# Order of the conditioning multiply-adds, and of the first item's passes, in a one-core fp32r block kernel

## The chip, the cores and the metric

The kernel runs on one NeuronCore of a Trainium2 chip. The metric is the device time of one execution in microseconds (us), the median over several runs. TensorE is called PE here, VectorE DVE, ScalarE ACT, GpSimd POOL and SyncE SP.

## What is computed

Two model blocks on one sequence of 512 tokens and 1024 channels, all in float32. Cut to what matters here:

```python
def _swiglu(h, w_gu, w_down):
    gate, up = jnp.split(h @ w_gu, 2, axis=-1)
    return (jax.nn.silu(gate) * up) @ w_down
...
x = x + 0.5 * _swiglu(_rmsnorm(x, ffn1_norm), ffn1_w_gu, ffn1_w_down)
h = _rmsnorm(x, mix_norm)
u_hy, u_rw, g_hy, g_rw = jnp.split(h @ w_in, split_at, axis=-1)
...
x = x + merged @ w_out
x = x + 0.5 * _swiglu(_rmsnorm(x, ffn2_norm), ffn2_w_gu, ffn2_w_down)
...
cond = jax.nn.silu(c)
ada = cond @ ada_w[l] + ada_b[l]
...
y = jnp.square(jax.nn.relu(h @ w1)) @ w2
x = x + g2[:, None, :] * rmsnorm(y, norm_g[l, 3])
```

`cond @ ada_w` and `cond @ kv_ada_w` are the conditioning: a vector of 1024 times a wide matrix. They depend on no token, so the kernel spreads them over other work. The rest (a Hyena branch, an RWKV-7 scan, an mLSTM, an attention) lies between the stages that the change touches.

## The kernel before

The text names functions and lines of the profiled kernel. Channels lie on the partitions; a weight matrix is processed by `dense` (L518), which is called five times: `ffn1`, `hy_in`, `mix`, `mlp0` and `mlp1`. Each call gets a list of steps: `Gemm` (a weight matrix), `Norm` (an RMS norm that makes the input of the next Gemm) and `Cut` (the same without a norm).

**Items.** `lay_out` (L430) cuts each Gemm into items of about 1 MB of weights: 8 blocks of 128 rows by two output tiles of 128 columns. Every product is made in three passes, because a float32 number is cut into a high and a low fp32r part: high weight by high input, high weight by low input, low weight by high input. So an item has 8 x 2 x 3 = 48 matmuls of 128 x 512 (L658, L660, L664). Two slots hold raw, high and low weights, so item i+2 uses the slots of item i, and also the PSUM banks of item i where a group is one item.

**What each engine does for an item i,** in program order:

- SP loads the raw weights of item n when item n-2 has its low part (L591 to L604).
- ACT: `take_out(i)` (silu of the gate tile, L757, or relu, L763), then `upper(i+2)`, the high part of the weights (L732), which waits for the last matmul of item i.
- DVE: `take_out(i)` (for swiglu and sqrelu two operations to a tile, L845 and L846; for "add" one, L861), then `lower(i+2)`, the low part of the weights (L836), and then, in a Gemm with a side job, `side_half(st, i)` (L887): four multiply-adds of one half of a conditioning block (L897, L900), each waiting for the one before.
- POOL: `side_load(st, i)` (L993, the DMA of L999), then the low part of item i's result (L1017), which waits for `take_out(i)`. `side_load` waits for `side_half(i-1)`, since there is one buffer `sraw`, and it stands in POOL's queue behind item i-1's low part.
- PE: the products; `bank_free` waits for DVE's `take_out(i-2)`; and after each even item but the first, and at the end of the Gemm, `side_sums` (L691): column sums of the accumulator `acc` (L697). A `side_half` of an even item starts `acc` anew and waits for the sums of the pair before, which PE makes behind the products of that same item.

Gemms with side jobs are: up (22 items, swiglu) and down (12 items, "add") of `ffn1` and of the second feed-forward in `mix`, each with blocks of 384 columns, and up1 (8 items, sqrelu) and down1 (8 items) of `mlp0`, with blocks of 256 columns. At the end of each, `side_take` (L904) adds the bias on DVE.

**The start of a stage.** The first item of a Gemm behind a Norm or Cut is "fresh": PE takes the input parts one by one as they come. It waits for the item's low weights before anything:

```python
for t in ts:
    bank_free(it, t)
pe.wait_ge(lo_ready, it.n + 1)
for k in ks:
    wait_hi(pe, st.parts, k)
    for t in ts:
        nc.tensor.matmul(ps[:, it.banks[t], :], w(h, k, t), xh[:, k, :], ...
        nc.tensor.matmul(ps[:, it.banks[t], :], w(l, k, t), xh[:, k, :], start=False, stop=False)
```

Where `dense` starts with a Norm or Cut, ACT makes `upper(items[0])` and DVE `lower(items[0])` ahead of the input parts (for a Norm that makes its own sums, ACT does it behind the squares). In `hy_in` the Norm is "known": the root was kept from an earlier stage, so its input parts need only x. The first items of `ffn1`, `hy_in`, `mlp0` and `mlp1` are fresh; that of `mix` is not.

Of the kernel before, what the change touches and what calls it, by code (L numbers as in the profile page):

```python
# [517 lines left out]
def dense(nc, e, tag, steps, buf):  # L518
# [6 lines left out]
    with ExitStack() as s:  # L525
# [80 lines left out]
        @block.tensor  # L606
        def _(pe):
            def bank_free(it, t):
                if it.first and it.earlier[t] is not None:
                    was, u = it.earlier[t]  # L610
                    if was.gemm.kind in ("copy", "tokens"):
                        pe.wait_ge(act_out, was.out[u])
                    else:
                        pe.wait_ge(dve_out, was.out[u])

            def products(it):
                st, h, l = it.gemm, slot(wh, it), slot(wl, it)
                xh, xl = st.x
                ks, ts = range(it.k0, it.k1), range(len(it.js))
                w = lambda of, k, t: of[:, k - it.k0, t * P:(t + 1) * P]  # L620
                pe.wait_ge(hi_ready, it.n + 1)
                if st.kind == "tokens":
                    for t in ts:
                        bank_free(it, t)
                        tok = slice(t * P, (t + 1) * P)
                        for k in ks:
                            nc.tensor.matmul(ps[:, t, :], xh[:, k, tok], h[:, k - it.k0, :],
                                             start=it.first and k == it.k0, stop=False)
                            nc.tensor.matmul(ps[:, t, :], xl[:, k, tok], h[:, k - it.k0, :], start=False, stop=False)
                        if t == 0:  # L630
                            pe.wait_ge(lo_ready, it.n + 1)
                        for k in ks:
                            last = nc.tensor.matmul(ps[:, t, :], xh[:, k, tok], l[:, k - it.k0, :], start=False,
                                                    stop=it.last and k == it.k1 - 1)
                        if it.last:
                            last.then_inc(tile_done, 1)
                elif it.fresh:
                    for t in ts:
                        bank_free(it, t)
                    pe.wait_ge(lo_ready, it.n + 1)  # L640
                    for k in ks:
                        wait_hi(pe, st.parts, k)
                        for t in ts:
                            nc.tensor.matmul(ps[:, it.banks[t], :], w(h, k, t), xh[:, k, :],
                                             start=it.first and k == it.k0, stop=False)
                            nc.tensor.matmul(ps[:, it.banks[t], :], w(l, k, t), xh[:, k, :], start=False, stop=False)
                    for k in ks:
                        wait_lo(pe, st.parts, k)
                        for t in ts:
                            last = nc.tensor.matmul(ps[:, it.banks[t], :], w(h, k, t), xl[:, k, :], start=False,  # L650
                                                    stop=it.last and k == it.k1 - 1)
                            if it.last and k == it.k1 - 1:
                                last.then_inc(tile_done, 1)
                else:
# [3 lines that stand above are left out]
                            nc.tensor.matmul(ps[:, it.banks[t], :], w(h, k, t), xh[:, k, :],  # L658
                                             start=it.first and k == it.k0, stop=False)
                            nc.tensor.matmul(ps[:, it.banks[t], :], w(h, k, t), xl[:, k, :], start=False, stop=False)  # L660
                        if t == 0:
                            pe.wait_ge(lo_ready, it.n + 1)
                        for k in ks:
                            last = nc.tensor.matmul(ps[:, it.banks[t], :], w(l, k, t), xh[:, k, :], start=False,  # L664
                                                    stop=it.last and k == it.k1 - 1)
                        if it.last:
                            last.then_inc(tile_done, 1)
                if not it.last:
                    last.then_inc(item_done, 1)

            def sum_tile(st, k):

                pe.wait_ge(squared, st.square[k])
                if k == 0 and st.order > 1:
                    pe.wait_ge(rooted, st.order - 1)
                for g in range(TT):
                    gs = slice(32 * g, 32 * g + 32)
                    last = nc.tensor.matmul(sums[gs, 0:P], e.ones[:, 0:32], sq[:, st.square[k] % 3, g * P:(g + 1) * P],
                                            start=k == 0, stop=k == st.n - 1)
                last.then_inc(summed, 1)  # L680

            def spread_root(st):
                pe.wait_ge(inverted, st.order)
                if st.saves > 0:
                    pe.wait_ge(saved, st.saves)
                for g in range(TT):
                    row = e.ident[:, 32 * g:32 * g + 1].to_broadcast([P, P])
                    last = nc.tensor.matmul(rs[:, g * P:(g + 1) * P], row, sd[:, 1, :], start=True, stop=True)
                last.then_inc(spread, 1)

            def side_sums(st, n):  # L691

                pe.wait_ge(side_step, DT * (st.side_at + n + 1))
                cols = st.side[1] // P
                for j in range(cols):
                    at = st.column_at + n * cols + j
                    last = nc.tensor.matmul(sps[:, at:at + 1], acc[:, j * P:(j + 1) * P], e.ones[:, 0:1],  # L697
                                            start=True, stop=True)
                last.then_inc(side_sum, 1)

            for st in steps:
                if isinstance(st, Gemm):
                    fed = st.feeds if isinstance(st.feeds, Norm) else None
                    for i, it in enumerate(st.items):
                        products(it)
                        if fed and i > 0 and st.items[i - 1].last:
                            for j in st.items[i - 1].js:
                                sum_tile(fed, j)
                        if st.side and i > 0 and i % 2 == 0:
                            side_sums(st, i // 2 - 1)  # L710
                    if fed:
                        for j in st.items[-1].js:
                            sum_tile(fed, j)
                    if st.side:
                        side_sums(st, len(st.items) // 2 - 1)
                elif isinstance(st, Norm) and not st.known:
                    if st.fed is None:
                        for k in range(st.n):
                            sum_tile(st, k)
                    spread_root(st)  # L720

        @block.scalar
        def _(act):
# [74 lines left out]
            for st in steps:  # L798
# [7 lines left out]
                if isinstance(st, Norm) and not st.known:  # L806
# [3 lines left out]
                    if started == 0:  # L810
                        upper(items[0])
                    root(st)
                elif started == 0:
                    upper(items[0])
                if st.kind == "parts" and (isinstance(st, Norm) or st.fed is None):
                    for k in range(st.n):
                        first_part(st, k)
                if isinstance(st, Norm) and st.root is not None and not st.known:
                    act.wait_ge(pieces, st.piece[-1])
                    nc.scalar.activation(st.root, rs[:, :], ACT.Copy).then_inc(saved, 1)  # L820
# [7 lines left out]
        def _(dve):  # L828
# [136 lines left out]
            for st in steps:  # L965
                if isinstance(st, Gemm):
                    for i, it in enumerate(st.items):
                        if it.last:
                            take_out(it)
                        if following(it) and not late(it):  # L970
                            lower(following(it))
                        if st.side:
                            side_half(st, i)
                    if st.side:
                        side_take(st)
                    continue
                if started == 0:
                    lower(items[0])
                if isinstance(st, Norm):
                    pieces_of(st)  # L980
                if st.kind == "parts":
                    for k in range(st.n):
                        if not st.on_pool[k]:
# [2163 lines left out]
```

## Time and profile before

| | |
|---|---|
| median of 3 runs | 3242.55 us (3241.94 to 3242.68) |
| the profiled execution, its own time | 3243.93 us |
| its span, first to last instruction | 3242.1 us |
| PE busy (matmuls; ends are modelled) | 2813.5 us, 87% of the span |
| DVE busy | 1592.8 us, 49% |
| ACT busy | 873.1 us, 27% |
| POOL busy | 400.5 us, 12% |
| mean granted PE clock | 0.916 of full speed |
| DMA | 272.78 MB, mean 84 GB/s |

Shares are averages over stages with different limits. In the stages of `dense` PE works without gaps through most items and waits at their starts and ends. A busy time of a matmul includes its way through the array: back-to-back matmuls of 128 x 512 start every 0.23 us at full clock though each is shown with 0.39 us.

### The profile page before, as it was taken

The numbers are of one execution on the slowest core, as the hardware profiler recorded it, in microseconds if no ns is written. First come the engines' busy times: TensorE is split into PE (matmuls) and PEld (weight loads), VectorE is DVE, ScalarE is ACT, GpSimd is POOL, SyncE is SP. The second block draws the span as 40 slices with busy tenths as digits, with TensorE's granted clock in tenths as the row PEclk, the third lists the DMA queues.
The fourth block names the chain that finished last, engine by engine and source line by source line (L and its number), as shares of the span: only waits on it lengthen the run. The fifth ranks groups of instructions, "written<-read, shape, count | busy, mean of one in ns | idle before, by whom it ended". The sixth has DMA issues, their size and how long they took to land. (4 is left out here: it accounts for less than half of the span.)

```text
span 3242.1 us, 40247 instructions
## 1 busy us (share of the span) xinstructions
PE 2813.5 (87%) x17297; PEld 2199.6 (68%) x17297; DVE 1592.8 (49%) x2116; ACT 873.1 (27%) x1114; POOL 400.5 (12%) x376
## 2 busy tenths in 40 slices
PE   7999997788587769999998979589999659889998
PEld 5887874777462458788876853368877446668886
DVE  5554456666655453565545224644263535353342
ACT  3221234111134112322213233332221333432221
POOL 1111001111001110111100001212030100021010
PEclk8999998899798789999998987789999779989999
DMA  5554530000020022355543310123243210223231
GB/s 159 160 159 153 163 100 21 3 3 3 28 73 26 0 65 85 98 162 168 167 141 123 100 34 2 52 65 107 95 137 121 53 44 2 78 67 103 91 104 52
DMA packets 267299, 272.78 MB, mean 84 GB/s; under 512 B 10559, under 2 KB 248102, under 8 KB 266927
## 3 DMA queue, kind: packets, MB, share of 16 engines
q1 hardware_dynamic: 251760, 208.32, 21.0%
q0 software_dynamic: 15360, 61.87, 5.8%
q8 instruction: 137, 2.24, 0.3%
q14 instruction: 42, 0.34, 0.0%
HBM read 268.07 MB, written 2.10 MB: 83 GB/s over the span
## 5 line engine op out<-in xcount | busy, mean ns | idle before, releaser
L836 DVE TENSOR_TENSOR mlp_wl<-mlp_raw,mlp_wh 128x2048 fp32r<-128x2048 f32 x74 | 189.9, 2566 | 290.7 <-ACT mlp_wh L732 290.7
L836 DVE TENSOR_TENSOR mix_wl<-mix_raw,mix_wh 128x2048 fp32r<-128x2048 f32 (+2 forms) x66 | 153.1, 2320 | 244.6 <-ACT mix_wh L732 244.5
L658 PE MATMUL mix_ps<-h_mix_hi,mix_wh 128*128 128x512 f32 x624 | 245.1, 393 | 9.2 <-ACT mix_wh L732 9.2
L660 PE MATMUL mix_ps<-h_mix_lo,mix_wh 128*128 128x512 f32 x624 | 243.7, 390 | 0.0
L732 ACT ACTIVATE mix_wh<-mix_raw 128x2048 fp32r<-128x2048 f32 (+2 forms) x66 | 117.6, 1781 | 246.0 <-PE mix_ps L664 162.1
L732 ACT ACTIVATE mlp_wh<-mlp_raw 128x2048 fp32r<-128x2048 f32 x74 | 140.5, 1899 | 154.0 <-PE mlp_ps L664 88.8
L658 PE MATMUL ffn_ps<-h_rw_hi,ffn_wh 128*128 128x512 f32 x448 | 175.2, 391 | 0.0
L660 PE MATMUL ffn_ps<-h_rw_lo,ffn_wh 128*128 128x512 f32 x448 | 174.3, 389 | 0.0
L664 PE MATMUL mix_ps<-h_mix_hi,mix_wl 128*128 128x512 f32 x624 | 154.2, 389 | 0.0
L658 PE MATMUL mlp_ps<-view,mlp_wh 128*128 128x512 f32 x384 | 150.1, 391 | 0.0
L660 PE MATMUL mlp_ps<-view,mlp_wh 128*128 128x512 f32 x384 | 149.5, 389 | 0.0
L836 DVE TENSOR_TENSOR ffn_wl<-ffn_raw,ffn_wh 128x2048 fp32r<-128x2048 f32 (+1 forms) x42 | 106.1, 2526 | 80.7 <-ACT ffn_wh L732 80.7
L658 PEld LDWEIGHTS mix_ps<-h_mix_hi,mix_wh 128*128 128x128 f32 x624 | 117.8, 189 | 34.2 <-ACT mix_wh L732 9.6
L1017 POOL TENSOR_TENSOR view<-mlp_f,view 128x512 fp32r<-128x512 f32 x64 | 86.4, 1351 | 424.6 <-DVE mlp_f L846 424.6
L660 PEld LDWEIGHTS mix_ps<-h_mix_lo,mix_wh 128*128 128x128 f32 x624 | 117.8, 189 | 24.1
L664 PEld LDWEIGHTS mix_ps<-h_mix_hi,mix_wl 128*128 128x128 f32 x624 | 117.1, 188 | 24.3
L732 ACT ACTIVATE ffn_wh<-ffn_raw 128x2048 fp32r<-128x2048 f32 (+1 forms) x42 | 78.7, 1874 | 177.2 <-PE ffn_ps L664 149.9
L658 PE MATMUL mlp_ps<-h_ml_hi,mlp_wh 128*128 128x512 f32 x296 | 115.7, 391 | 0.0
L660 PE MATMUL mlp_ps<-h_ml_lo,mlp_wh 128*128 128x512 f32 x296 | 115.3, 389 | 0.0
L658 PE MATMUL mlp_ps<-h_mla_hi,mlp_wh 128*128 128x512 f32 x288 | 112.3, 390 | 0.0
L845 DVE SCALAR_TENSOR_TENSOR view<-mlp_ps,mlp_f 128x512 fp32r<-128x512 f32 x64 | 44.2, 691 | 138.3 <-ACT mlp_f L763 138.3
L660 PE MATMUL mlp_ps<-h_mla_lo,mlp_wh 128*128 128x512 f32 x288 | 112.1, 389 | 0.0
(560 smaller groups left out, 6111.5 us busy)
## 6 DMA issues: line engine op xcount, KB each, us to landing
mlp_raw<-in_mlp_w SPq DMA_DIRECT2D x64, 1024.0 KB, 5.3
ffn_sraw<-in_ada_w POOLq DMA_DIRECT2D x34, 768.0 KB, 5.3
ffn_raw<-in_ffn_w_gu SPq DMA_DIRECT2D x44, 512.0 KB, 5.2
mix_raw<-in_ffn_w_gu SPq DMA_DIRECT2D x44, 512.0 KB, 4.6
mix_sraw<-in_ada_w POOLq DMA_DIRECT2D x22, 768.0 KB, 5.2
mix_raw<-in_a_w_in SPq DMA_DIRECT2D x12, 1024.0 KB, 5.3
mix_sraw<-in_kv_ada_w POOLq DMA_DIRECT2D x12, 768.0 KB, 4.9
ffn_raw<-in_w_in SPq DMA_DIRECT2D x8, 1024.0 KB, 5.3
```

The source lines that it names most:

```text
L658: nc.tensor.matmul(ps[:, it.banks[t], :], w(h, k, t), xh[:, k, :], start=it.first and k == it.k0, stop=False)
L660: nc.tensor.matmul(ps[:, it.banks[t], :], w(h, k, t), xl[:, k, :], start=False, stop=False)
L664: last = nc.tensor.matmul(ps[:, it.banks[t], :], w(l, k, t), xh[:, k, :], start=False, stop=it.last and k == it.k1 - 1)
L732: nc.scalar.activation(slot(wh, it), slot(raw, it), ACT.Copy).then_inc(hi_ready, 1)
L836: nc.vector.tensor_tensor(slot(wl, it), slot(raw, it), slot(wh, it).bitcast(F32), ALU.subtract)\
L845: nc.vector.scalar_tensor_tensor(st.dst[0][:, j, :], ps[:, bank, :], op0, f[:, u % 2, :], op1, ALU.mult)
L1017: nc.gpsimd.tensor_tensor(d, f[:, 2 + u % 2, :], st.dst[0][:, j, :].bitcast(F32), ALU.subtract).then_inc(low, 1)
```

## The change

Four edits, all in `dense`.

1. PE, first item of a call (`it.n == 0`) if fresh: the wait for the low weights moves behind the pass of high weights by high inputs, and the low weights by high inputs become a pass of their own, which comes second.
2. ACT, `dense` that starts with a known Norm (only `hy_in`): `upper(items[0])` moves from ahead of the eight high input parts to behind the fourth.
3. DVE, the same stage: `lower(items[0])` moves behind the eight products of the Norm (`pieces_of`).
4. DVE, every item with a side job: `side_half` moves from behind `lower` to ahead of `take_out`.

```diff
@@ products, fresh item
                     for t in ts:
                         bank_free(it, t)
-                    pe.wait_ge(lo_ready, it.n + 1)
+                    if it.n > 0:
+                        pe.wait_ge(lo_ready, it.n + 1)
                     for k in ks:
                         wait_hi(pe, st.parts, k)
                         for t in ts:
                             nc.tensor.matmul(ps[:, it.banks[t], :], w(h, k, t), xh[:, k, :],
                                              start=it.first and k == it.k0, stop=False)
-                            nc.tensor.matmul(ps[:, it.banks[t], :], w(l, k, t), xh[:, k, :], start=False, stop=False)
+                            if it.n > 0:
+                                nc.tensor.matmul(ps[:, it.banks[t], :], w(l, k, t), xh[:, k, :], start=False, stop=False)
+                    if it.n == 0:
+                        pe.wait_ge(lo_ready, 1)
+                        for k in ks:
+                            for t in ts:
+                                nc.tensor.matmul(ps[:, it.banks[t], :], w(l, k, t), xh[:, k, :], start=False, stop=False)
@@ scalar
-                elif started == 0:
+                elif started == 0 and not isinstance(st, Norm):
                     upper(items[0])
                 if st.kind == "parts" and (isinstance(st, Norm) or st.fed is None):
                     for k in range(st.n):
                         first_part(st, k)
+                        if started == 0 and isinstance(st, Norm) and st.known and k == st.n // 2 - 1:
+                            upper(items[0])
@@ vector
                     for i, it in enumerate(st.items):
+                        if st.side:
+                            side_half(st, i)
                         if it.last:
                             take_out(it)
                         if following(it) and not late(it):
                             lower(following(it))
-                        if st.side:
-                            side_half(st, i)
                     if st.side:
                         side_take(st)
                     continue
-                if started == 0:
+                known = isinstance(st, Norm) and st.known
+                if started == 0 and not known:
                     lower(items[0])
                 if isinstance(st, Norm):
                     pieces_of(st)
+                if started == 0 and known:
+                    lower(items[0])
```

DVE's queue in the first items of `ffn1`'s up Gemm, before (`wl` is the low weights, `acc` the conditioning accumulator, `ffn_f` what ACT's silu wrote and the second result part; a line "x3" is three of them):

```order
L836 TENSOR_TENSOR ffn_wl<-ffn_raw,ffn_wh 128x2048
L897 TENSOR_SCALAR ffn_acc<-ffn_sraw,cond 128x384
L900 SCALAR_TENSOR_TENSOR ffn_acc<-ffn_sraw,cond,ffn_acc 128x384 x3
L845 SCALAR_TENSOR_TENSOR view_194<-ffn_ps,ffn_f 128x512
L846 SCALAR_TENSOR_TENSOR ffn_f<-ffn_ps,ffn_f 128x512
L836 TENSOR_TENSOR ffn_wl<-ffn_raw,ffn_wh 128x2048
L900 SCALAR_TENSOR_TENSOR ffn_acc<-ffn_sraw,cond,ffn_acc 128x384 x4
```

The same queue with the change (line numbers are 9 higher; the first line is the low part of item 1's weights):

```order
L845 TENSOR_TENSOR ffn_wl<-ffn_raw,ffn_wh 128x2048
L906 TENSOR_SCALAR ffn_acc<-ffn_sraw,cond 128x384
L909 SCALAR_TENSOR_TENSOR ffn_acc<-ffn_sraw,cond,ffn_acc 128x384 x3
L854 SCALAR_TENSOR_TENSOR view_194<-ffn_ps,ffn_f 128x512
L855 SCALAR_TENSOR_TENSOR ffn_f<-ffn_ps,ffn_f 128x512
L845 TENSOR_TENSOR ffn_wl<-ffn_raw,ffn_wh 128x2048
L909 SCALAR_TENSOR_TENSOR ffn_acc<-ffn_sraw,cond,ffn_acc 128x384 x4
```

The cyclic order of the three groups is the same; what moved is where an item begins. Before, the four lines on `acc` between two pairs of L845 and L846 belong to the item whose pair is ahead of them; now they (L906, L909) belong to the item whose pair is behind them, and that pair can't run until they have.

POOL's queue in the same place with the change, which is as before but for line numbers (the DMA loads the conditioning block, the other operation is the low part of an item's result):

```order
L1011 DMA ffn_sraw<-in_ada_w 128x4x384
L1029 TENSOR_TENSOR view_195<-ffn_f,view_194 128x512
L1011 DMA ffn_sraw<-in_ada_w 128x4x384
L1029 TENSOR_TENSOR view_195<-ffn_f,view_194 128x512
L1011 DMA ffn_sraw<-in_ada_w 128x4x384
```

Nothing moved here: each load stands behind the low part of the item before, as it did.

ACT's queue at the start of `hy_in` with the change (before, the first `hy_in_wh` stood ahead of all eight `h_mix_hi`; the last two lines are the take-out of item 0):

```order
L787 ACTIVATE h_mix_hi<-view_8977 128x512 x4
L739 ACTIVATE hy_in_wh<-hy_in_raw 128x2048
L787 ACTIVATE h_mix_hi<-view_8977 128x512 x4
L739 ACTIVATE hy_in_wh<-hy_in_raw 128x2048
L755 ACTIVATE view_8971<-hy_in_ps,cols 128x512
L759 ACTIVATE view_8972<-hy_in_ps 128x512
```

Four input parts are now made ahead of the weights. PE's first 32 matmuls there alternated between `hy_in_wh` and `hy_in_wl`; now sixteen read `hy_in_wh`, and then sixteen `hy_in_wl`.

## Rows read from the trace of the kernel before

**Rows 1.** waits of PE over the whole execution: waited for, us in total, times, longest.

```profile
PE mlp_ps L644 <- DVE mlp_wl L836: 42.7, 2, 32.2
```

**Rows 2.** timeline, ffn1's up Gemm, items 1 to 3: start, duration (us), instruction, [idle before].

```profile
63.31 2.57 DVE L900 SCALAR_TENSOR_TENSOR ffn_acc<-ffn_sraw,cond,ffn_acc 128x384 f32<-128x384 f32 x4
...
69.25 0.73 PE L697 MATMUL ffn_sps<-ones,ffn_acc 128*128 128x1 f32 x6
69.45 0.69 DVE L845 SCALAR_TENSOR_TENSOR view<-ffn_ps,ffn_f 128x512 fp32r<-128x512 f32 x1 [3.58 <-PE ffn_ps L664]
70.06 0.68 DVE L846 SCALAR_TENSOR_TENSOR ffn_f<-ffn_ps,ffn_f 128x512 f32<-128x512 f32 x1
71.46 2.81 DVE L836 TENSOR_TENSOR ffn_wl<-ffn_raw,ffn_wh 128x2048 fp32r<-128x2048 f32 x1 [0.72 <-ACT ffn_wh L732]
74.19 0.41 DVE L897 TENSOR_SCALAR ffn_acc<-ffn_sraw,cond 128x384 f32<-128x384 f32 x1
74.64 1.93 DVE L900 SCALAR_TENSOR_TENSOR ffn_acc<-ffn_sraw,cond,ffn_acc 128x384 f32<-128x384 f32 x3
...
70.83 1.28 POOL L1017 TENSOR_TENSOR view<-ffn_f,view 128x512 fp32r<-128x512 f32 x1 [3.89 <-DVE ffn_f L846]
76.86 0.77 POOL L999 DMA_DIRECT2D ffn_sraw<-in_ada_w  x1 [4.74 <-DVE ffn_acc L900]
```

**Rows 3.** timeline, the end of ffn1's up Gemm (item 21).

```profile
283.03 0.69 DVE L845 SCALAR_TENSOR_TENSOR view<-ffn_ps,ffn_f 128x512 fp32r<-128x512 f32 x1 [4.72 <-PE ffn_ps L664]
...
290.10 1.44 PE L697 MATMUL ffn_sps<-ones,ffn_acc 128*128 128x1 f32 x6 [7.10 <-DVE ffn_acc L900]
```

**Rows 4.** timeline, mlp0's up0 Gemm, item 0, DVE and then POOL.

```profile
2174.99 0.69 DVE L845 SCALAR_TENSOR_TENSOR view<-mlp_ps,mlp_f 128x512 fp32r<-128x512 f32 x1 [2.13 <-ACT mlp_f L763]
...
2177.39 2.42 DVE L836 TENSOR_TENSOR mlp_wl<-mlp_raw,mlp_wh 128x2048 fp32r<-128x2048 f32 x1
2177.62 3.34 POOL L1017 TENSOR_TENSOR view<-mlp_f,view 128x512 fp32r<-128x512 f32 x1
```

**Rows 5.** DVE at 40 us; loads' landing: ffn1, those of 40, 55, 276 us, mlp0.

```profile
38.09 4.26 DVE L918 TENSOR_TENSOR h_rw_lo<-view,h_rw_hi 128x512 fp32r<-128x512 f32 x4
...
DMA to landing us min/median/max: 4.9/5.3/6.7
...
ffn_sraw<-in_ada_w POOLq DMA_DIRECT2D x1, 768.0 KB, 5.4
...
ffn_sraw<-in_ada_w POOLq DMA_DIRECT2D x1, 768.0 KB, 6.7
...
ffn_sraw<-in_ada_w POOLq DMA_DIRECT2D x1, 768.0 KB, 4.9
...
DMA to landing us min/median/max: 3.9/4.6/5.8
```

**Rows 6.** column sums of mlp0 (first and last start), and the end of its up1 Gemm.

```profile
L697 PE MATMUL mlp_sps<-ones,mlp_acc x32: 168/250/370, 2370.2 to 2530.6; 128*128 128x1 f32 x32
...
2431.66 2.03 DVE L900 SCALAR_TENSOR_TENSOR mlp_acc<-mlp_sraw,cond,mlp_acc 128x256 f32<-128x256 f32 x4
2433.75 1.01 PE L697 MATMUL mlp_sps<-ones,mlp_acc 128*128 128x1 f32 x4 [7.46 <-DVE mlp_acc L900]
```

**Rows 7.** timeline, start of hy_in.

```profile
887.82 1.91 ACT L732 ACTIVATE hy_in_wh<-hy_in_raw 128x2048 fp32r<-128x2048 f32 x1 [13.66 <-DMA hy_in_raw<-in_w_in]
...
893.53 0.77 PE L644 MATMUL hy_in_ps<-h_mix_hi,hy_in_wh 128*128 128x512 f32 x1 [25.71 <-ACT h_mix_hi L780]
```

**Rows 8.** timeline, start of mlp0.

```profile
2091.01 4.25 ACT L786 ACTIVATE h_ml_hi<-view 128x512 fp32r<-128x512 f32 x8
...
2093.53 0.76 PE L644 MATMUL mlp_ps<-h_ml_hi,mlp_wh 128*128 128x512 f32 x1 [32.18 <-DVE mlp_wl L836]
```

**Rows 9.** timeline, the end of ffn1's down Gemm.

```profile
422.17 0.83 PE L697 MATMUL ffn_sps<-ones,ffn_acc 128*128 128x1 f32 x6 [1.40 <-DVE ffn_acc L900]
...
423.44 0.95 DVE L936 RECIPROCAL ffn_sd<-ffn_sd 128x128 f32<-128x128 f32 x1
```

## The prediction

> **What bounds the kernel now.** I read the page first: PE is busy 87% of the span, everything else half of it or less, so what counts is where PE waits and what comes last there. Then the waits of PE: it waits for the low weights of a first item twice [rows 1]; the start of `hy_in` and the ends of the Gemms with a side job show in the timeline. In the middle of a Gemm there is no wait worth the name: 19 items of the up Gemm take 283.03 - 69.45 = 213.6 us, 11.24 us each [rows 2, 3]. So the question for each edit is what it does to a start or an end, and whether a chain on another engine becomes longer than an item.
>
> **Starts.** In `hy_in` the raw weights land, ACT makes the high part at 887.82 in 1.91 us, DVE the low part behind it, then the first product of the Norm and its high part, and PE starts at 893.53 [rows 7]. With the change the products and four high input parts are made while the weights are still on their way, and PE needs only the high weights: 887.82 + 1.91 + 0.1 = 889.8. After that PE doesn't wait again: the first matmul of a part takes 0.77 us there [rows 7], and a part is made in 0.53 us (eight in 4.25 [rows 8]). Saved: 3.7 us. In `mlp0` ACT starts the high input parts at 2091.01, 4.25 / 8 = 0.53 us each and the first ends at about 2091.6, while PE waits for the low weights until 2093.53 [rows 8]: saved 1.9 us, and the same in `mlp1`, the second of the two waits [rows 1]. In `ffn1` PE waits for the Norm, not for the weights: nothing. The low weights take DVE 2.4 us [rows 4] and are ready long before PE's second sixteen. Sum of the starts: -7.5 us.
>
> **The side job moved ahead of the take-out.** This is the edit that decides. At first sight it only gains: at the end of up PE waits 7.10 us for the last multiply-add, because it comes behind take-out and low weights [rows 3], and 7.46 us in `mlp0` [rows 6]. But it closes a loop that was open. The load of the next conditioning block stands in POOL's queue behind the low part of this item's result; that waits for the take-out; the take-out now waits for this item's multiply-adds; and these wait for their load. Nothing in this loop waits for PE once it is late. Its links for a swiglu item:
>
> - four multiply-adds: 74.19 to 76.57 = 2.38 us for an even item, 2.57 us for an odd one [rows 2];
> - take-out: 69.45 to 70.74 = 1.29 us, and POOL starts 0.1 us later [rows 2];
> - the low part on POOL: 1.28 us [rows 2], but that is with DVE idle or behind it. DVE's low weights wait for ACT there until 71.46, so POOL is first, and DVE takes 2.81 us beside it. With the change an even item's take-out ends at least 4.2 us behind the item (0.7 us of column sums, 2.4, 1.3), when ACT's high weights are long ready, so DVE starts the low weights in the same moment and is 0.2 us ahead of POOL. The trace has this very sequence once in `mlp0`: DVE starts at 2177.39 and takes 2.42 us, POOL starts at 2177.62 and takes 3.34 us instead of 1.28 [rows 4]. I take 3.34;
> - issue to landing of the load: 5.3 us median, 4.9 to 6.7; of the 17 loads of this Gemm that I read one by one, from the one of 55 us to the one of 276 us, the mean is 5.5 [rows 5]. A chain adds means, so I take 5.5; the weight load is now issued 1.2 us ahead of it, not 2.6;
> - 0.15 us for POOL's step to the load and DVE's start on it, an estimate.
>
> A link is 2.38 + 1.29 + 0.1 + 3.34 + 5.5 + 0.15 = 12.8 us from an even to an odd item, 13.0 us back: 12.85 against the 11.24 of PE. So the side job falls behind by 1.6 us an item. After some five or six items the take-out of item i ends later than PE is done with item i+1, and then PE waits for its banks; for the end that makes no difference, since PE can't go on to down before the last sums. The loop's last free point is item 2, whose multiply-adds start behind the sums at 69.25 + 0.73 = 70.0 [rows 2]. From there 10 even and 9 odd links are 10 x 12.76 + 9 x 12.95 = 244.2 us, and the last multiply-adds 2.57: 316.7, where PE's last sums started at 290.10 [rows 3]. **+26.6 us**, and the same in the second feed-forward: +53.2. The bounds are those of the load: with 4.9 us 19 x 0.6 = 11.4 us less, +15.2 each; with 6.2 us, nearer to the longest rows, 13.3 more, +39.9 each. With 5.3, the median, it is 3.8 less.
>
> Up1 of `mlp0` has eight items, two tiles each: multiply-adds 2.0, take-out 2177.39 - 2174.99 + 0.1 = 2.5 us, POOL's second low part 0.1 + 3.34 [rows 4], load 4.9 (median 4.6, range 3.9 to 5.8 [rows 5]; seven loads have this mean), 0.15: 13.0 us. From item 2, 2370.2 + 0.6 = 2370.8 [rows 6], five links and 2.03 us lead to 2437.8, where it was 2433.75: +4.1 us, bounds +1 and +8.
>
> **Where the side job has no such loop.** In down and down1 POOL has nothing but the loads, so a link is multiply-adds plus load, 2.4 + 5.5 + 0.4 = 8.3 us, less than an item, and the even items stay tied to PE's sums. There the last multiply-adds are ready before the item ends, DVE's two additions come next at once, and the root's reciprocal, which stood behind sums that had waited 1.40 us [rows 9], comes earlier; the take-out of the first tile now comes late, behind the multiply-adds, and eats about 0.3 us. I take -1.1, -1.1 and -0.8, in sum -3.0 us; bounds -5 and, if the last load is late, +3. DVE's added delay of the low weights (2.4 us of 11) costs nothing: the next use is an item later.
>
> **Sum**, against the profiled execution: 3243.93 - 7.5 + 53.2 + 4.1 - 3.0 = 3290.7 us. The median of the runs is 1.4 us below that execution, so 3289 us, 1.4% slower.
>
> **A rule against the trace.** The load issued at 40 us had DVE busy with operations on two SBUF inputs all around it (38.09 to 42.35) and landed in 5.4 us, as the others do [rows 5]. The Trainium skill, page "SBUF — State Buffer", section "SBUF: two separate sides", states that a DMA from GpSimd's queue gets no descriptors written while DVE holds the shared port in a two-port mode. By that rule the loads of the down Gemms, now issued right when DVE starts its low weights, would land some 2 us later.
>
> **Rivals.**
>
> 1. *POOL keeps its turn* (faster). If the low part of the result starts ahead of DVE's low weights, or isn't held up, it takes 1.28 us, the link is 10.7 us and below PE's 11.24: the loop never closes, item 21's multiply-adds end at 272.0 + 10.7 + 2.57 = 285.3, and PE saves 4.8 us at each swiglu end and about 5 in `mlp0`. Total 3242.5 - 7.5 - 9.6 - 5 - 3: 3217 us. It decides at a hold-up of POOL below some 0.5 us. For it: POOL was first in every side item so far. Against: rows 4, and that the order of the queues fixes who is first. 11%.
> 2. *The loads get longer* since weights and conditioning now travel together: above 6.2 us the sum is over 3320 us, each 0.1 us more adds 4 us. Against: the transfers were overlapping before. 9%.
> 3. *DVE holds up the loads of down*: the last multiply-adds end 1.5 to 2 us behind the last item instead of ahead, the ends of down and down1 lose 1 us each instead of gaining one: +6, 3295 us. This is the rule above; the load of 40 us speaks against it. 4%.
> 4. *Shorter loads*, at or below 4.9 us, since the load now starts with DVE idle: below 3262 us, in the extreme nothing but the starts' gain against a small loss. 4%, half of it within 0.2%.
>
> My forecast has the remaining 72%.
>
> **Numbers.** A measurement of this kernel can tell about 0.2%, 6.5 us, from no change. The range follows the load's landing from 4.9 to 6.2 us: -22.8 - 2.5 and +26.6 + 3 around 3289, so 3264 to 3319, and I take 3262 to 3322. Rival 1 and parts of 2 and 4 lie outside. Faster 0.12 (rival 1 and a little of 4), same 0.02, slower 0.86.
>
> **What would show it.** In the profile after: POOL's L1017 of the up Gemms near 3.3 us instead of 1.28; in the later items of up, PE idle 1 to 2 us before an item, waiting for DVE's L846; PE's wait for the last sums of up near 13 us instead of 7; some 317 us instead of 290 for the last sums of `ffn1`'s up. PE's first matmul of `hy_in` 3.7 us earlier in its stage. I am wrong if L1017 stays at 1.28 us, or if up ends before its old time.

## The result, and the profile after

| | before | after |
|---|---|---|
| median of the runs | 3242.55 us | 3341.27 us (3329.38 to 3345.36, 4 runs) |
| the profiled execution, its own time / span | 3243.93 / 3242.1 us | 3345.36 / 3343.4 us |
| PE busy | 2813.5 us, 87% | 2845.3 us, 85% |
| POOL busy | 400.5 us | 492.2 us |

The change makes the kernel slower: ratio 1.0300, 95% interval 1.0285 to 1.0314. Forecast were 3289 us and at most 3322. The sign was right, the size half of what came.

In the new kernel the take-out stands in L854 and L855, the low weights in L845, the multiply-adds in L906 and L909, the load in L1011, POOL's low part in L1029, the column sums in L704. First the waits of PE:

```profile
PE ffn_ps L665 <- DVE ffn_f L855: 26.9, 15, 3.8
PE mix_sps L704 <- DVE mix_acc L909: 22.3, 7, 13.5
PE hy_in_ps L645 <- ACT hy_in_wh L739: 21.9, 1, 21.9
PE mix_ps L665 <- DVE mix_f L855: 17.6, 15, 4.1
PE ffn_sps L704 <- DVE ffn_acc L909: 16.7, 5, 14.6
PE mlp_sps L704 <- DVE mlp_acc L909: 15.3, 1, 15.3
```

Two kinds are new: PE waits at the start of items for the take-out (L665), and its wait for the last sums of an up Gemm has doubled, from 7 to 14 or 15 us. Waits in the middle and at the end of an up Gemm are what a closed loop of the side job would leave. The loop is read link by link in `ffn1`'s up, DVE first (start, length, what ended the idle time):

```profile
59.79 2.58 DVE L909 SCALAR_TENSOR_TENSOR ffn_acc<-ffn_sraw,cond,ffn_acc 128x384 f32<-128x384 f32 x4 [8.31 <-DMA ffn_sraw<-in_ada_w]
62.29 0.68 DVE L854 SCALAR_TENSOR_TENSOR view<-ffn_ps,ffn_f 128x512 fp32r<-128x512 f32 x1
62.89 0.68 DVE L855 SCALAR_TENSOR_TENSOR ffn_f<-ffn_ps,ffn_f 128x512 f32<-128x512 f32 x1
63.49 2.28 DVE L845 TENSOR_TENSOR ffn_wl<-ffn_raw,ffn_wh 128x2048 fp32r<-128x2048 f32 x1
73.75 0.42 DVE L906 TENSOR_SCALAR ffn_acc<-ffn_sraw,cond 128x384 f32<-128x384 f32 x1 [7.98 <-DMA ffn_sraw<-in_ada_w]
...
87.86 1.27 DVE L909 SCALAR_TENSOR_TENSOR ffn_acc<-ffn_sraw,cond,ffn_acc 128x384 f32<-128x384 f32 x2 [8.34 <-DMA ffn_sraw<-in_ada_w]
```

and POOL and SP beside it:

```profile
63.66 3.26 POOL L1029 TENSOR_TENSOR view<-ffn_f,view 128x512 fp32r<-128x512 f32 x1 [10.30 <-DVE ffn_f L855]
66.87 0.77 POOL L1011 DMA_DIRECT2D ffn_sraw<-in_ada_w  x1
77.42 3.25 POOL L1029 TENSOR_TENSOR view<-ffn_f,view 128x512 fp32r<-128x512 f32 x1 [9.78 <-DVE ffn_f L855]
80.62 0.77 POOL L1011 DMA_DIRECT2D ffn_sraw<-in_ada_w  x1
...
65.80 14.75 SPq L599 DMA_DIRECT2D ffn_raw<-in_ffn_w_gu  x4
```

DVE's low weights start 0.17 us ahead of POOL's low part (63.49, 63.66), and POOL takes 3.26 us, near the 3.34 of rows 4. SP issues the weight load when the low weights are done, at 65.80 (the four issues of that row are those of two items); the conditioning load follows 1.07 us later, at 66.87, and DVE has it at 73.75, 6.88 us on. The link from 59.79 to 73.75 is 2.50 + 1.37 + 3.21 + 6.88 = 13.96 us, the next, to 87.86, 14.11. The profile page's row of the loads and the line of POOL's low part agree:

```profile
ffn_sraw<-in_ada_w POOLq DMA_DIRECT2D x34, 768.0 KB, 6.9
...
L1029 POOL TENSOR_TENSOR view<-ffn_f,view x22: 2962/3252/3258, 49.4 to 344.3; 128x512 fp32r<-128x512 f32 x22
```

The end of that Gemm, for [rows 3]:

```profile
340.43 2.58 DVE L909 SCALAR_TENSOR_TENSOR ffn_acc<-ffn_sraw,cond,ffn_acc 128x384 f32<-128x384 f32 x4 [7.58 <-DMA ffn_sraw<-in_ada_w]
...
343.06 1.44 PE L704 MATMUL ffn_sps<-ones,ffn_acc 128*128 128x1 f32 x6 [14.56 <-DVE ffn_acc L909]
```

From 59.79 to 340.43 lie 20 links, 14.03 us each. The last sums start at 343.06 instead of 290.10.

In this Gemm the loop is closed from item 0 on. In the second feed-forward it closes at item 2, whose multiply-adds still wait for PE's column sums; up to there POOL starts ahead of DVE's low weights (its first two low parts take 1.28 us):

```profile
1453.91 0.42 DVE L906 TENSOR_SCALAR mix_acc<-mix_sraw,cond 128x384 f32<-128x384 f32 x1 [6.71 <-PE mix_sps L704]
```

From there to the last multiply-adds at 1723.21 are 19 links of 14.17 us.

How far the kernel is behind, place by place:

| place | before | after | behind | since the place before |
|---|---|---|---|---|
| last sums of `ffn1` up | 290.10 | 343.06 | +53.0 | +53.0 |
| root at the end of `ffn1` down | 423.44 | 475.23 | +51.8 | -1.2 |
| first matmul of `hy_in` | 893.53 | 939.76 | +46.2 | -5.6 |
| bias behind the second up | 1629.2 | 1728.8 | +99.6 | +53.4 |
| bias behind the second down | 1761.4 | 1857.3 | +95.9 | -3.7 |
| first matmul of `mlp0` | 2093.53 | 2190.44 | +96.9 | +1.0 |
| last sums of `mlp0` up1 | 2433.75 | 2538.83 | +105.1 | +8.2 |
| end of the span | 3242.1 | 3343.4 | +101.3 | -3.8 |

### The profile page after: what moved, and what is told of

It is laid out like the page before. It is cut to its first block and busy times, and to the rows that moved or that the text cites. A ratio compares the mean times of both kernels' runs of the same rounds, so it can differ in the third digit from the quotient of the medians.

```text
span 3343.4 us, 40244 instructions
## 1 busy us (share of the span) xinstructions
PE 2845.3 (85%) x17297; PEld 2210.6 (66%) x17297; DVE 1561.3 (47%) x2116; ACT 872.4 (26%) x1114; POOL 492.2 (15%) x376
## 5 line engine op out<-in xcount | busy, mean ns | idle before, releaser
L845 DVE TENSOR_TENSOR mlp_wl<-mlp_raw,mlp_wh 128x2048 fp32r<-128x2048 f32 x74 | 186.3, 2518 | 258.1 <-ACT mlp_wh L739 258.1
L665 PE MATMUL mix_ps<-h_mix_hi,mix_wh 128*128 128x512 f32 x624 | 254.3, 408 | 26.6 <-DVE mix_f L855 17.6
L667 PE MATMUL mix_ps<-h_mix_lo,mix_wh 128*128 128x512 f32 x624 | 252.0, 404 | 0.0
L845 DVE TENSOR_TENSOR mix_wl<-mix_raw,mix_wh 128x2048 fp32r<-128x2048 f32 (+2 forms) x66 | 142.1, 2153 | 190.1 <-ACT mix_wh L739 190.0
L665 PE MATMUL ffn_ps<-h_rw_hi,ffn_wh 128*128 128x512 f32 x448 | 183.4, 409 | 27.0 <-DVE ffn_f L855 26.9
L667 PE MATMUL ffn_ps<-h_rw_lo,ffn_wh 128*128 128x512 f32 x448 | 181.5, 405 | 0.0
L1029 POOL TENSOR_TENSOR view<-mlp_f,view 128x512 fp32r<-128x512 f32 x64 | 98.5, 1543 | 461.3 <-DVE mlp_f L855 461.3
L665 PEld LDWEIGHTS mix_ps<-h_mix_hi,mix_wh 128*128 128x128 f32 x624 | 123.0, 197 | 56.7 <-ACT mix_wh L739 16.2
L665 PE MATMUL mlp_ps<-view,mlp_wh 128*128 128x512 f32 x384 | 150.1, 391 | 0.0
L909 DVE SCALAR_TENSOR_TENSOR ffn_acc<-ffn_sraw,cond,ffn_acc 128x384 f32<-128x384 f32 x119 | 73.6, 619 | 104.0 <-DMA ffn_sraw<-in_ada_w 100.3
L665 PEld LDWEIGHTS ffn_ps<-h_rw_hi,ffn_wh 128*128 128x128 f32 x448 | 88.6, 198 | 49.2 <-ACT ffn_wh L739 15.4
L909 DVE SCALAR_TENSOR_TENSOR mix_acc<-mix_sraw,cond,mix_acc 128x384 f32<-128x384 f32 x119 | 73.6, 619 | 100.6 <-DMA mix_sraw<-in_ada_w 85.8
L665 PE MATMUL mlp_ps<-h_ml_hi,mlp_wh 128*128 128x512 f32 x296 | 115.7, 391 | 0.0
L665 PE MATMUL mlp_ps<-h_mla_hi,mlp_wh 128*128 128x512 f32 x288 | 112.3, 390 | 0.0
```

Source lines behind the costliest of these rows:

```text
L845: nc.vector.tensor_tensor(slot(wl, it), slot(raw, it), slot(wh, it).bitcast(F32), ALU.subtract)\
L909: ins = nc.vector.scalar_tensor_tensor(acc[:, 0:cols], sraw[:, kk, 0:cols], cond[:, k:k + 1], acc[:, 0:cols], ALU.mult, ALU.add)
L1029: nc.gpsimd.tensor_tensor(d, f[:, 2 + u % 2, :], st.dst[0][:, j, :].bitcast(F32), ALU.subtract).then_inc(low, 1)
```

## The experiments

The kernel before gave 3242.59 us (17 runs) beside the first four runs and 3242.35 us (7 runs) beside the last three. My theory after the result: the loop is the one forecast, and it is longer than forecast since the conditioning load shares the DMA engines with a weight load issued 1.1 us ahead of it. Rivals: the edits of the starts have a part in the loss; or POOL's hold-up alone decides, and the loads' length follows from something else.

**1. The starts alone** (edits 1 to 3; the side job stays behind the low weights).

```diff
-                        if st.side:
-                            side_half(st, i)
                         if it.last:
                             take_out(it)
                         if following(it) and not late(it):
                             lower(following(it))
+                        if st.side:
+                            side_half(st, i)
```

> The three edits of the starts without the moved side job. Theory (all of the loss is the side job's loop): 3242.5 - 7.5 = 3235 us, within 3231 to 3238; hy_in's PE starts some 3.7 us earlier in its stage, mlp0's and mlp1's 1.9 us each. Rival (a start edit costs something too): 3243 us or more.

Measured: 3234.32 us (8 runs), ratio 0.9970 (0.9955 to 0.9986). The starts gain 8.3 us by the medians (between 4.5 and 14.6 us by the interval), where the sum had 7.5. PE's waits fell by 3.4 us in `hy_in` (25.7 to 22.3), 1.8 in `mlp0` (32.2 to 30.4) and 1.7 in `mlp1` (10.5 to 8.8), 6.9 us together.

**2. The side job alone** (edit 4 in the kernel before).

```diff
                     for i, it in enumerate(st.items):
+                        if st.side:
+                            side_half(st, i)
                         if it.last:
                             take_out(it)
...
-                        if st.side:
-                            side_half(st, i)
```

> Only the side job moved ahead of the take-out, starts as before. Theory: the whole loss plus what the starts gave back, 3341 + 8 = 3349 us, within 3338 to 3358; POOL's low parts of up stay at 3.25 us and the loads at about 6.9 us. Rival (the start edits carry part of the loss): under 3335 us.

Measured: 3344.99 us, ratio 1.0313 (1.0297 to 1.0328), 102.4 us more than before, with a median landing of 6.9 us for the 22 loads of each up Gemm. POOL's low parts there take 3.05 us in the mean, since the first two of each are still at 1.28. The whole loss is edit 4's. (The starts give back 3.7 us here by the two medians, where 8 were expected; the spread of the runs doesn't tell these apart.)

**3. The load ahead of the low part.** The changed kernel, but POOL issues the load of item i+1 before it waits for item i's take-out. POOL's hold-up may stay; it only leaves the loop.

```diff
-                        if st.side:
-                            side_load(st, i)
+                        if st.side and i == 0:
+                            side_load(st, 0)
+                        if st.side and i + 1 < len(st.items):
+                            side_load(st, i + 1)
                         for u, t in zip(it.use, range(2)):
```

> The changed kernel, with POOL's load of the next conditioning block put ahead of the low part of the item's result, so that it waits for the multiply-adds alone. Theory (the loop through take-out and POOL is the loss): a link is 2.4 + 0.1 + 7 = 9.5 us, below an item's 11.24, so the loss goes and the ends of up gain 5 us each: 3205 to 3222 us, faster than before. Rival (it is the later take-outs and low weights themselves, or the side job's own work, that hold PE up): 3300 us or more. Second rival (the longer landing, 7 us, comes back as a late end): 3225 to 3245.

Measured: 3201.23 us (3198.88 to 3203.34), ratio 0.9869 (0.9852 to 0.9885): faster than both kernels and below what was expected. POOL and SP in its trace, in the same item, and its last sums of `ffn1`'s up:

```profile
71.86 0.77 POOL L1011 DMA_DIRECT2D ffn_sraw<-in_ada_w  x1 [11.54 <-DVE ffn_acc L909]
72.85 3.25 POOL L1031 TENSOR_TENSOR view<-ffn_f,view 128x512 fp32r<-128x512 f32 x1 [0.22 <-DVE ffn_f L855]
...
74.98 0.99 SPq L599 DMA_DIRECT2D ffn_raw<-in_ffn_w_gu  x2
...
281.92 0.73 PE L704 MATMUL ffn_sps<-ones,ffn_acc 128*128 128x1 f32 x6
```

The low part still takes 3.25 us in every other item (in the items between, DVE waits for ACT's high weights, POOL is first and takes 1.28 us; the mean is 2.26), so the hold-up as such costs nothing that these runs show: run 5, without any, isn't faster. The load is now 3.1 us ahead of the weights instead of 1.1 behind, in the items between 4.7 to 4.9, and lands in 5.1 us (median). The last sums come without a wait.

**4. The weight load behind.** The changed kernel; SP issues an item's weights only when the conditioning load beside them has landed. This takes away the shared transfer and leaves POOL's hold-up in the loop.

```diff
+                if it.n >= 4:
+                    side = items[it.n - 4].gemm
+                    i = it.n - 4 - side.items[0].n
+                    if side.side and i + 1 < len(side.items):
+                        sp.wait_ge(side_in, 16 * (loads_earlier + side.half_at + i + 2))
                 ks = slice(it.k0, it.k1)
```

> The changed kernel, with SP's weight load held until the conditioning load issued beside it has landed; nothing else moved. Theory (the landing of 6.9 us instead of 5.5 is the two transfers sharing the DMA engines): landing 5.0 to 5.5 us, a link 1.5 us shorter, 19 links twice and 5 in mlp0: 3341 - 57 - 5 = about 3280 us, within 3265 to 3295. Rival (the load lands late because of what POOL or DVE do at its issue): landing stays near 6.9 us and the time at 3330 to 3350.

Measured: 3249.55 us (10 runs), ratio 1.0024 (1.0014 to 1.0033), 92 us less than the changed kernel, where 61 less were expected.

```profile
76.64 0.77 POOL L1016 DMA_DIRECT2D ffn_sraw<-in_ada_w  x1
...
81.62 2.58 DVE L914 SCALAR_TENSOR_TENSOR ffn_acc<-ffn_sraw,cond,ffn_acc 128x384 f32<-128x384 f32 x4 [6.07 <-DMA ffn_sraw<-in_ada_w]
...
93.78 0.42 DVE L911 TENSOR_SCALAR ffn_acc<-ffn_sraw,cond 128x384 f32<-128x384 f32 x1 [6.19 <-DMA ffn_sraw<-in_ada_w]
...
302.57 1.44 PE L709 MATMUL ffn_sps<-ones,ffn_acc 128*128 128x1 f32 x6 [11.41 <-DVE ffn_acc L914]
```

With nothing beside it the load takes 81.62 - 76.64 = 4.98 us, and a link 93.78 - 81.62 = 12.16 us, 1.9 less than in the changed kernel; POOL's part is still 3.0 to 3.3 us in 20 of the 22 items. The expectation missed two things: a link is shorter by 1.9 us, not 1.5, and item 2's multiply-adds start at 69.77 instead of 73.75. Together they are 19 x 1.9 + 4.0 = 40 us at the end of this Gemm (302.57 instead of 343.06), where 28.5 were expected. The loop is still longer than PE's 11.24 us: the sums wait 11.4 us and start at 302.57. So the 6.9 us came from the weight load beside it.

**5. POOL first.** The changed kernel; DVE starts the low weights of item i+2 only when POOL has made item i's low part.

```diff
                         if following(it) and not late(it):
+                            if st.side and it.use:
+                                dve.wait_ge(low, it.use[-1])
                             lower(following(it))
```

> The change, but DVE starts the low weights of item i+2 only when POOL has made item i's low part, so POOL isn't held up. My theory (two terms made the link 14.05 us: POOL's 3.25 us and the load's 6.9 us): POOL's low part of the result is back at 1.28 us, the link is 14.05 - 1.97 = 12.1 us if the landing stays at 6.9 us, still above PE's 11.24, and up of ffn1 ends near 70.0 + 19 x 12.1 + 2.6 = 302 us; in all about 3257 us. The weight load then starts some 1.3 us later too and may stretch the load less: down to 3220. Rival (my first rival of the prediction, POOL alone decides): 3217 us. Rival (POOL doesn't matter): 3341.

Measured: 3205.43 us (3204.83 to 3208.95), ratio 0.9887 (0.9873 to 0.9902). That is 136 us less than the changed kernel and 52 less than I expected. Of the figures named, the 3217 us of "POOL alone decides" came nearest; why it was too high stands below.

```profile
73.17 2.29 DVE L845 TENSOR_TENSOR ffn_wl<-ffn_raw,ffn_wh 128x2048 fp32r<-128x2048 f32 x1 [1.41 <-POOL view L1031]
...
71.85 1.28 POOL L1031 TENSOR_TENSOR view<-ffn_f,view 128x512 fp32r<-128x512 f32 x1 [11.13 <-DVE ffn_f L855]
73.08 0.77 POOL L1013 DMA_DIRECT2D ffn_sraw<-in_ada_w  x1
...
75.48 0.99 SPq L599 DMA_DIRECT2D ffn_raw<-in_ffn_w_gu  x2
```

POOL is back at 1.28 us, and DVE's 1.41 us of waiting cost nothing. My error was in the order of the loads: with POOL first, its load (73.08) goes out 2.4 us *ahead* of the weights (75.48), and it lands in 5.1 us. What stretches instead is the weight load, 5.7 us median in `ffn1`'s up against 4.7 before, and it has an item's time to spare.

**6. Both** (5 and 4 together).

> The change with both terms taken away: POOL ahead of DVE's low weights (1.28 us), and the weight load of an item waits until the side load beside it has landed. My theory: a link is 12.0 us (as the weights-behind run had it) less 1.97 = 10.1 us, below PE's 11.24, so the loop never closes and what is left is the gain of the edits: 3242.6 - 8.3 (starts, as measured) and 5 to 8 us at each of the ends of up, up1: 3200 to 3217 us, as the run with the load ahead of the low part. If something else lengthens the loop, it stays above 3230.

Measured: 3208.44 us (3206.54 to 3209.28), as expected. Once POOL isn't held up, SP's wait gives nothing more. The four kernels make a square: changed 3341.3, weights behind 3249.6, POOL first 3205.4, both 3208.4. Either measure takes away the long landing; only "POOL first" takes away the hold-up as well.

**7. The side job and POOL's new order, without the starts** (2 and 3 together).

> The kernel before with the side job moved ahead of the take-out (edit 4 alone) and with POOL issuing the next load ahead of the low part; the three edits of the starts are left out. If starts and side job add up, this is the 3201.2 us of the run with all of them plus the 8.3 us that the starts were worth alone: 3209.5 us (3206 to 3213). If the starts give more or less beside a free side job, it is outside that.

Measured: 3209.16 us (3203.32 to 3211.89), as expected: starts and side job add up.

## Why the prediction was right and wrong

**Right: the mechanism.** The loop closed as described, POOL's low part went to 3.25 us (3.34 taken) in all but the first two items of the second feed-forward, DVE was 0.2 us ahead, up's last sums wait 14.6 us (some 13 forecast), and PE waits in the later items of up for DVE's L855 (L846 before). The gains also came: `ffn1` down's end -1.2 us (-1.1 taken), and the starts, 8.3 us in run 1 (7.5).

**Wrong: "so I take 5.5", the landing of the load in the loop.** It took 6.88 and 7.24 us in the two links read above, where the sum has 5.5 and 0.15 for DVE's start. The forecast's end of up was 70.0 + 19 links + 2.57 = 316.7; the trace has 340.43 + 2.58 = 343.0, 26.3 us later. Of these, 19 x (14.03 - 12.85) = 22.4 us is the length of a link, all of it the load (1.4 us longer in the mean), since the other terms were taken 0.2 us too long together. The rest is **"the loop's last free point is item 2, at 70.0"**: item 1's load was already one of the slow ones, so item 2's multiply-adds began at 73.75, 3.75 us late. This second error isn't general. In the second feed-forward of the same trace, and in `ffn1` of run 2 (69.67), item 2 was free as forecast. There all of the excess is the links: from item 2's start to the last sums the second feed-forward falls 51.9 us behind, not 26.6, and 19 x (14.17 - 12.85) = 25.1. In `mlp0`'s up1 it is less, +8.2 against +4.1: its five links from 2468.10 to 2536.73 are 13.7 us instead of 13.0, with loads that take 5.6 to 6.7 us where the sum had 4.9 and 0.15.

The error in reasoning is in two sentences. The sum says that "the weight load is now issued 1.2 us ahead of it, not 2.6", and draws nothing from it; rival 2 dismisses longer loads since "the transfers were overlapping before". Both treat overlap as yes or no. At 2.6 to 2.8 us the weight load (4.7 us from issue to landing, in the profile before) has more than half of its time behind it when the conditioning load is issued; at 1.1 us it has a quarter, and the later load pays. Rival 2, at 9%, is what happened: its price, 4 us of time for each 0.1 us of load, times the 1.2 us by which a link was longer, gives 3289 + 47 = 3336 us, near the 3341 measured. In a loop, every term is multiplied by the number of links (here 19, twice), so a bound drawn at 6.2 us, inside the range of single landings that rows 5 show (up to 6.7), was too tight. That 3336 comes so near is in part luck: the price takes neither the late start in `ffn1` nor what the stages between gave back.

**Wrong: rival 1's size.** With POOL's turn kept the forecast was 3217 us; 3205.4 were measured. The wait at the end of up costs more than its length, and the granted clock shows why. PE in the kernel before, around the wait of 7.10 us [rows 3] (window; length, PE busy, granted clock as a share of full speed, DMA share, GB/s):

```profile
283.00:290.00 7.00, 0.00 (x0) 0.86 0.17 48
290.00:294.00 4.00, 3.90 (x12) 0.50 0.94 285
294.00:298.00 4.00, 4.00 (x17) 0.89 0.16 61
298.00:302.00 4.00, 4.00 (x19) 1.00 0.00 0
```

and in the run with the load ahead of the low part, where there is no wait:

```profile
281.80:286.00 4.20, 4.20 (x23) 1.00 0.02 5
286.00:290.00 4.00, 4.00 (x19) 1.00 0.83 239
```

Behind the wait PE runs for 4 us at the lower of its two levels (1.2 instead of 2.4 GHz) and for a part of the next 4: 4 x 0.50 + 4 x 0.11 = 2.4 us lost, the longer sums (1.44 instead of 0.73 us) among it. In run 1, behind a wait of 7.10 us too, the lower level lasts longer and costs 7.43 x 0.50 = 3.7 us:

```profile
288.57:296.00 7.43, 7.43 (x21) 0.50 0.57 176
```

This accounts for the 11.9 us by which `ffn1` down ends earlier in run 3 than in run 1 (411.5 against 423.4): the last sums start 6.65 us earlier (281.92 against 288.57), the way from them to the sums ahead of down's last is 3.6 us shorter (114.7 against 118.3), and down's end gives 1.6. Three such ends, at 2.4 to 3.7 us, are 7 to 11 us of the 12 that rival 1 missed. Run 5, the kernel that rival 1 describes, still waits 1.7 us at this end, and its clock behind the wait stays at 1.00. In the changed kernel this term hides: the wait is longer (14.56 us), the slow start behind it much the same (0.50 in the first 4 us, 0.84 in the next).

**The starts.** `hy_in`'s wait fell by 3.8 us (25.7 to 21.9; 3.7 taken), yet the stage's first matmul comes 5.6 us earlier against the end of `ffn1` down. The other 1.8 us lie ahead of the stage. SP issues its first weights 0.25 us behind the last operation of DVE in the RWKV stage, and from the end of `ffn1` down to that issue pass 458.9 us before, 457.2 in the changed kernel, 454.6 in run 1 and 455.6 in run 2, which has no edit of the starts. Between 600 and 800 us, where no edit touches the work, the granted clock is 0.93 before and 1.00 in run 1. So that part is a difference between single executions and not the starts. In `mlp0` the wait fell from 32.18 to 31.33 us, 0.9 instead of 1.9, because the first weights landed 0.9 us later in that execution (high weights 6.97 us behind SP's issue, 6.06 before); from the start of the high weights to PE's first matmul it is 2.57 us instead of 4.34, 1.8 saved. Of the 2.6 us more than taken at the second down's end, 1.4 belong to the place that the table names: the bias behind the second up now comes behind DVE's low weights, so by the last sums (1725.84 against 1627.68) that place is 98.2 us behind, not 99.6. The other 1.2 us stay open.

**The rule on DVE and GpSimd's queue.** In `ffn1`'s down DVE starts low weights 0.7 us behind the issue of a load (388.65 and 387.94 in the changed kernel), and the loads of this Gemm land in 5.1 us, the median before and after. There is no hold-up by 2 us. But this doesn't test the rule, and the load of 40 us in the prediction didn't either. The Trainium skill, page "SBUF — State Buffer", section "SBUF: two separate sides", states it for DVE in a 2-port performance mode, and says further down that a `tensor_tensor`, which is what DVE's low weights and low input parts are, has no such mode and wasn't seen to stall a DMA. So rival 3 had applied the rule to an operation that it doesn't cover; the trace agrees with the section, 5.1 us beside DVE's subtraction as before. For POOL's own arithmetic the trace agrees with the shared port that the section describes: 1.28 us alone, 3.25 us behind DVE's subtraction of two SBUF inputs, and 1.28 us again where POOL starts first, as in [rows 2], with DVE's low weights at 2.81 us instead.

## What to carry to other kernels

Before moving work ahead of something in a queue, follow who issues the next load of that work. If the load stands behind the result of the item, the move closes a loop, and every term of it counts once per link: take its landing under the new neighbours, not the old median. Here the cure was to issue the load as soon as its buffer is free, ahead of the wait for the take-out; it turned a loss of 99 us into a gain of 41.

When two loads are under way together, in these runs the order of their issue decides which one stretches (the second: 6.9 instead of 5.1 us for the conditioning, 5.7 instead of 4.7 for the weights), so put the one without slack first.

## What the hardware showed

- 768 KB from POOL's queue land in about 5.0 us alone (run 4), 5.1 us in the median when a 1 MB weight load follows 2.4 us or more behind (runs 3 and 5), 5.3 us when one was issued 2.6 to 2.8 us ahead (single ones 4.9 to 6.7), and 6.9 us when it is 1.1 us ahead (single ones 6.2 to 8.1 in `ffn1`'s up).
- Two elementwise operations that start 0.2 us apart, DVE first: POOL's goes from 1.28 to 3.25 us, and it ends 1.1 us behind DVE's 2.28. With POOL first and DVE behind it, POOL takes 1.28 and DVE 2.81 us [rows 2]; with DVE waiting for POOL's end, 1.28 and 2.29 us.
- A wait of PE of 7.1 us costs 2.4 us (kernel before) or 3.7 us (run 1) more behind it, at the lower clock. Behind a wait of 1.7 us (run 5) the clock stays at full.
